# Prompt attention: the softmax weights scaled by diagonals in the turning product, the diagonals built by GpSimd

## The reference, cut to what matters

```python
s = jnp.einsum('bqhgd,bkhd->bhgqk', qf, win_k.astype(f32))
p_win = masked_softmax(s - m * delta.astype(f32), wmask)
o_win = jnp.einsum('bhgqk,bkhd->bqhgd', p_win, win_v.astype(f32))
gate = jax.nn.sigmoid(gts.astype(f32))
o = gate[..., 0:1] * o_cmp + gate[..., 1:2] * o_sel + gate[..., 2:3] * o_win
```

## Time and profile before

| what | us |
| --- | --- |
| median of 3 runs | 2677.11 (2675.2 to 2685.92) |
| the profiled execution, its own time | 2676.88 |
| its span in the trace | 2675.2 |
| TensorE busy in the span | 1895.4 |
| VectorE busy | 1095.8 |
| GpSimd busy | 739.6 |
| ScalarE busy | 439.3 |

### The profile page before, as it was taken

One profiled execution on the slowest core, in us unless ns is written; L12 is line 12 of the kernel. 1 busy time (PEld: TensorE's weight loads), 2 busy tenths in 40 slices (PEclk: granted clock), 3 DMA queues, 4 the chain that ended last, 5 costly groups with the idle time before them and its releaser, 6 DMA issues.

```text
span 2675.2 us, 30528 instructions
## 1 busy us (share of the span) xinstructions
PE 1895.4 (71%) x11821; PEld 1225.1 (46%) x11821; DVE 1095.8 (41%) x1929; ACT 439.3 (16%) x978; POOL 739.6 (28%) x599
## 2 busy tenths in 40 slices
PE   5799999988889934677649897672764116565673
PEld 2477777868768934566536564121221101111120
DVE  2200002426583597676750127018777860000014
ACT  0100000122271212343400101110221000000011
POOL 1000000000010034443452223337546853222234
PEclk8899999999999976787769998766887556777785
DMA  9889997434047689999999999999999999999997
GB/s 385 288 312 347 330 330 239 143 96 156 11 142 233 204 307 416 411 413 412 413 421 402 418 417 417 414 402 405 390 381 410 379 390 406 401 414 421 422 421 315
DMA packets 283277, 911.81 MB, mean 341 GB/s; under 512 B 22254, under 2 KB 158498, under 8 KB 209978
## 3 DMA queue, kind: packets, MB, share of 16 engines
q0 software_dynamic: 78384, 569.78, 52.2%
q1 hardware_dynamic: 176354, 304.77, 32.0%
q10 hardware_dynamic: 28396, 35.35, 3.7%
HBM read 901.18 MB, written 17.21 MB: 343 GB/s over the span
## 4 chain that ended last, share of the span: by engine, by line
DMA 43%; PE 34%; DVE 12%; POOL 7%; issue 3%; ACT 1%; ACTq 0%; SPq 0%; DVEq 0%; POOLq 0%; PEldq 0%
DMA sb_ring<-in_peer_v_dram,sb_modT 19%; DMA sb_ring<-in_peer_u_dram,sb_dist 18%; PE ps L418 14%; POOL sb_ring L2650 7%; DVE sb_ring L2120 4%; PE ps L2572 3%; DMA sb_ring<-in_w_ada_dram 3%; PE ps L212 3%; PE ps L1873 2%; DMA sb_ring<-in_cache_sel_kv_dram 1%; PE ps L2328 1%; PE ps L2291 1%; PE ps L751 1%; PE ps L761 1%; DMA sb_pT<-in_cache_sel_kv_dram 1%
## 5 line engine op out<-in xcount | busy, mean ns | idle before, releaser
L2120 DVE SCALAR_TENSOR_TENSOR sb_ring<-sb_ring,sb_pT 128x2048 f32<-128x2048 f32 x264 | 602.6, 2294 | 244.2 <-DMA sb_ring<-in_peer_u_dram,sb_dist 199.7
L2650 POOL DMA_INDIRECT sb_ring<-in_peer_u_dram,sb_dist x256 | 423.4, 1654 | 532.7 <-DVE sb_ring L2120 352.3
L2572 PE MATMUL ps<-sb_ring,sb_xT 128*32 128x512 f32 x2048 | 343.5, 767 | 192.1 <-DMA sb_ring<-in_peer_v_dram,sb_modT 188.9
L2650 POOL DMA_INDIRECT sb_ring<-in_peer_v_dram,sb_modT x256 | 255.6, 998 | 561.5 <-PE ps L2572 543.7
L418 PE MATMUL ps<-sb_hT,sb_ring 128*128 128x264 f32 x1664 | 374.8, 388 | 0.0
L418 PEld LDWEIGHTS ps<-sb_hT,sb_ring 128*128 128x128 f32 x1664 | 315.5, 190 | 65.3 <-issue 13.0
L2572 PEld LDWEIGHTS ps<-sb_ring,sb_xT 128*32 128x32 f32 x2048 | 49.9, 121 | 426.3 <-DMA sb_ring<-in_peer_v_dram,sb_modT 381.0
L2407 PE MATMUL ps<-sb_ident,sb_ring 128*128 128x128 f32 x512 | 103.7, 359 | 135.9 <-DMA sb_ring<-in_cache_cmp_kv_dram 109.9
L1672 PE MATMUL ps<-sb_work,sb_pT 128*64 128x512 f32 x160 | 99.4, 708 | 98.0 <-ACT sb_work L1560 63.0
L2407 PEld LDWEIGHTS ps<-sb_ident,sb_ring 128*128 128x128 f32 x512 | 78.0, 184 | 159.4 <-DMA sb_ring<-in_cache_cmp_kv_dram 127.9
L2461 ACT ACTIVATE sb_pT<-ps 128x256 f32<-128x256 f32 x256 | 127.5, 661 | 97.0 <-PE ps L2407 96.8
(11 more groups left out here) (586 smaller groups left out, 2383.7 us busy)
## 6 DMA issues: line engine op xcount, KB each, us to landing
sb_ring<-in_w_ada_dram SPq DMA_DIRECT2D x48, 2048.0 KB, 11.1
sb_ring<-in_w_in_dram SPq DMA_DIRECT2D x26, 2048.0 KB, 14.3
sb_ring<-in_peer_wq_dram SPq DMA_DIRECT2D x19, 1024.0 KB, 13.3
sb_ring<-in_cache_cmp_kv_dram SPq DMA_DIRECT2D x68, 256.0 KB, 12.1
sb_ring<-in_w_out_dram SPq DMA_DIRECT2D x8, 2048.0 KB, 8.5
sb_ring<-in_cache_cmp_kv_dram ACTq DMA_DIRECT2D x60, 256.0 KB, 10.6
sb_ring<-in_w_out_dram SPq DMA_DIRECT2D x13, 1024.0 KB, 9.8
sb_pT<-in_peer_wq_dram SPq DMA_DIRECT2D x13, 1024.0 KB, 15.8
```

The source lines that it names most:

```text
L2120: dve.scalar_tensor_tensor(R3(rows), R3(rows), 1.0, h2r[t] if t < NT else R3(h2w), ALU.mult, ALU.mult, accum_out=(dots if t < NT else dots ...
L2572: mm = pe.matmul(bank(G % 2)[32 * q:32 * q + 32, :], w, rows[:, 512 * q:512 * q + 512], start=j == 0, stop=j == last)
L2650: pool.indirect_dma_start(rbuf[e % NBUF], None, io["peer_u" if kind == "u" else "peer_v"][0], bass.IndirectOffsetOnAxis(index, 0)).then_in ...
```

## The change

VectorE no longer scales the weights. It only computes gate / sum for the three branches (for tile 0 the compressed one is also multiplied by the first column of the mask, which is 0 for queries that have no complete block). GpSimd builds from them three diagonal matrices of 128x128 side by side (`dg`, two buffers), as the identity times the three columns. TensorE multiplies the unscaled exponentials by the diagonal of their branch: a product that turns and scales at once, where a transpose against the identity stood. `pool_states` is now called inside GpSimd's loop, behind the diagonals of item 8.

```diff
+        dg = [v3(old(3 * P), 0, 3, P), osq.rearrange("p h c -> p (h c)")[:, 0:3 * P].rearrange("p (r c) -> p r c", r=3)]
@@ pool_att
+            pool.wait_ge(sem("o_sums"), 1)
+            for i in range(N_ATT):
+                pool.wait_ge(sem("p_ready"), i + 1)
+                if i >= 2:
+                    pool.wait_ge(sem("pt_T"), i - 1)
+                pool.tensor_tensor(dg[i % 2], B1(ident[:], 3), B2(stat[1][i % 3], P), ALU.mult).then_inc(sem("diag_ready"), 1)
+                if i == HEADS:
+                    pool_states(pool)
@@ pe_kv
-                pe.wait_ge(sem("p_ready"), i + 1)
+                pe.wait_ge(sem("diag_ready"), i + 1)
                 if i >= 1:
                     pe.wait_ge(sem("pt_moved"), i)
                 for k in range(2 * (t + 1)):
-                    pe.transpose(bank(4 + i % 2)[:, k * P:(k + 1) * P], s[:, k * P:(k + 1) * P], ident[:])
-                pe.transpose(bank(6)[0:NCP, 0:P], s[:, 512:520], ident[:]).then_inc(sem("pt_T"), 1)
+                    pe.matmul(bank(4 + i % 2)[:, k * P:(k + 1) * P], s[:, k * P:(k + 1) * P], dg[i % 2][:, 1 + k // (t + 1), :], start=True, stop=True)
+                pe.matmul(bank(6)[0:NCP, 0:P], s[:, 512:520], dg[i % 2][:, 0, :], start=True, stop=True).then_inc(sem("pt_T"), 1)
@@ dve_kv
                 step(dve, c, dve.reciprocal(total, total))
-                step(dve, c, dve.tensor_tensor(total, total, gates[:, t * 24 + 3 * h:t * 24 + 3 * h + 3], ALU.mult))
-                two = s[:, 0:2 * nk].rearrange("p (a k) -> p a k", a=2)
-                dve.tensor_tensor(two, two, B2(total[:, 1:3], nk), ALU.mult)
-                dve.scalar_tensor_tensor(s[:, 512:520], s[:, 512:520], total[:, 0:1], cseen3[:, t, :], ALU.mult, ALU.mult).then_inc(sem("p_ready"), 1)
+                if t == 0:
+                    step(dve, c, dve.tensor_tensor(total[:, 0:1], total[:, 0:1], cseen3[:, t, 0:1], ALU.mult))
+                dve.tensor_tensor(total, total, gates[:, t * 24 + 3 * h:t * 24 + 3 * h + 3], ALU.mult).then_inc(sem("p_ready"), 1)
@@ gpsimd stream
-            for stage in (pool_setup, pool_att_consts, pool_delta, pool_att, pool_states, pool_samp, pool_peer):
+            for stage in (pool_setup, pool_att_consts, pool_delta, pool_att, pool_samp, pool_peer):
```

More of the change, by code:

```diff
@@ L75 @@
     top_ready exp_done pt_part dve_steps samp_consts samp_ready x1_ready keys_T keys_ready rows_out
-    rows_mm keyscores keyscore_mm halves_done top_diff peer_consts experts_ready ids_here keys_in
+    diag_ready rows_mm keyscores keyscore_mm halves_done top_diff peer_consts experts_ready ids_here keys_in
     rest_in0 w2b_in
```

## The result

The changed kernel takes 2695.93 us (median of 14 runs, 2688.16 to 2708.25) against 2677.65 for the kernel before (14 runs, 2673.82 to 2685.92). The ratio is 1.0071, with a 95% interval of 1.0057 to 1.0084: slower by 19 us (15 to 22), where I had forecast 6 and a range that ended at 2693.

What follows compares the result with a forecast made beforehand. VectorE's work and the round trip between engines, nearly level, were taken to bound the attention stage. First half 1.4, seam 0.1, pause 0.6 and second half 4.05 sum to 6.15 us on 2676.88: 2683 us, range 2675 to 2693.

Steps and rivals of the forecast that it cites:

- What bounds the stage: Prompt attention, second half: VectorE's work (3.66 us a turn) and the round trip through the engines (3.60) are 0.06 apart.
- GpSimd's product: 128x384 diagonal product each turn: 0.87 us, bounds 0.53 to 1.82; gate product to turning 1.15 us instead of 1.08.
- TensorE's term: Turning by full products takes two 0.11 us records each, not one: 0.55 us more a turn, 0.33 in first half.
- First half: Tile 0 of the prompt attention: delays carried head by head make the move behind turning 7 late by 1.4 us.
- Second half at full clock: Tile 1: round trip 4.22 us instead of 3.60, seven turns +4.05 us; its first turn adds +0.1.
- The pause by the state transfers: GpSimd's two DMA issues of the decode states delay the tenth diagonal: +0.6 us, once.
- the states' lateness: States leave some 8.3 us later, delaying output-weight loads, but these arrive before the projection needs them: no cost.
- Sum at full clock: Attention stage: 1.4 + 0.1 + 0.6 + 4.05 = 6.15 us longer.
- The clock: TensorE's granted clock in the attention stage and projection: the forecast had no term for it.
- Pass-through: A shift of the attention stage's end was taken as a shift of the kernel's end, one to one.
- Rival 3: A load or gather behind the attention stage hides its 6 us lengthening: 2677 us; chance 0.15.
- Rival 2: GpSimd's product far slower, at its upper bound or held up by VectorE's traffic: 2693.6 us; chance 0.14.

Runs made afterwards that it cites:

- experiment 6: Kernel before, with TensorE's outputs of the previous item put ahead of the wait for the weights: 2678.00 us, ratio 1.0013 to the kernel before.
- Experiment 1: Kernel before, with turning by full products with the identity instead of transposes, VectorE's scaling kept: 2690.79 us, ratio 1.0047 to the kernel before.
- experiment 5: Changed kernel, with seven unread identity products ahead of TensorE's wait for the diagonals in each of the last two items: 2692.09 us, ratio 1.0054 to the kernel before.
- experiment 2: Changed kernel, with turning by transposes that still wait for GpSimd's unread diagonals, scaling left out: 2686.01 us, ratio 1.0033 to the kernel before.
- 12: Repeat of experiment 2 (changed kernel with transposes kept, scaling left out): ratio 1.0013 to the kernel before.
- experiment 8: Kernel before, outputs first, with outer-product diagonals from the fourth on and the delta heads' output gate moved from VectorE to GpSimd: 2676.32 us, ratio 0.9994.

## Why the prediction was wrong

- *What bounds the stage:* right. VectorE's work and the round trip were level; experiment 6 shows the first, and every item after the change is a round trip.
- *GpSimd's product:* 0.83 us against 0.87, and 1.12 from gate product to turning against 1.15. Right: the slope between the 32 columns of the earlier trace rows and these 384 is 1.67 ns a column, where I had 1.78. In items 14 and 15 the product took 1.03 and 1.01 us, which I had not foreseen. The 2.6 cycles an element of the Trainium skill (GPSIMD Engine Reference, section 3.1) are, as an estimate at the 1.2 GHz that it names, 0.83 us for 384 elements. The trace agrees with that at this size; at 32 columns the same estimate is 0.07 us, where the earlier trace rows have 0.242. My 1.0, from the Trainium skill's figure for 2048 columns in the same section, was too high.
- *TensorE's term:* this is the step that failed first: "five per turn in the second half cost 5 x 0.11 = 0.55 us more". It cost 0.90. I divided the 0.89 us of the chain by eight records, but the chain cuts a group where its neighbour ends. The weight loader's rows were there to be read. Before the change:

```profile
818.91 0.42 PEld L1212 LDWEIGHTS ps<-sb_ident,sb_work 128*128 128x128 f32 x4 [1.72 <-DVE sb_work L1330]
819.30 0.09 PEld L1213 LDWEIGHTS ps<-sb_ident,sb_work 128*8 128x8 f32 x1
819.40 0.97 PEld L1194 LDWEIGHTS ps<-sb_work 128*128 128x128 f32 x8
820.50 0.29 PEld L1195 LDWEIGHTS ps<-sb_work,sb_pT 8*128 8x128 f32 x2
```

Four transposes take 0.39 us and the fifth, of 8 columns, 0.10; four products take 1.10 (819.40 to 820.50). After the change:

```profile
809.73 0.97 PEld L1221 LDWEIGHTS ps<-sb_pT,sb_work 128*128 128x128 f32 x8 [0.48 <-POOL sb_pT L1123]
810.82 0.10 PEld L1222 LDWEIGHTS ps<-sb_pT,sb_work 128*8 128x8 f32 x2
811.13 0.97 PEld L1203 LDWEIGHTS ps<-sb_work 128*128 128x128 f32 x8 [0.22 <-issue]
```

The four turning products take 1.09 and the one of 8 columns 0.31, with the loader idle for 0.22 of it. So a product is 0.27 to 0.31 us against 0.10, 1.40 against 0.49 for the five. Experiment 1 shows it alone: 3.60 + 0.90 = 4.50. The Trainium skill (TensorE: Matmul & The Clock Gate, Terms) calls the transpose mode four times faster for fp32. The trace does not agree: here it is 2.8 times (1.10 us against 0.39 for four).
- *First half:* 2.9 us by the move in item 7, where I had +1.4. The same term, for the most part: turning to outputs grew by 0.68 us, not 0.33 (778.76 to 779.72 by the weight loader's rows, where it was 0.28). Experiment 1, without GpSimd, has 2.0 of the 2.9.
- *Second half at full clock:* seven items took 32.3 us (experiment 5) where they took 25.49, so +6.9, where I had +4.05 and 0.6 for the pause. TensorE's term is 7 x 0.90 = 6.3 of it, and the longer products of GpSimd in the last two items 0.4. Item 8 adds another 0.4, where I had 0.1.
- *The pause by the state transfers:* forecast 0.6, measured 0.13, because the items are longer than the issues; and the states' lateness cost nothing, as forecast.
- *Sum at full clock:* +10.2 in the stage (experiment 5) against +6.15. The mechanism of this part was right and the TensorE term too small.
- *The clock:* missing altogether, and the second step that failed: a term that I had put at nothing without a reason. The stage's end and the projection lost 4.6 + 1.8 us to the lower clock. I had noted that it was 1.00 throughout before, and took that as given for a program with longer waits.
- *Pass-through:* right as far as the timed 19 us show it; the rest is 1792.7 after 1792.6, but moves by up to 9 us from trace to trace. Rival 3 is out, since its time was 2677. Rival 2's time (2693.6) came nearest by luck: GpSimd's product was not slow.
- The two parts make 16.7 us of the measured 19 (15 to 22). The remaining 2 are within the interval, and no run settles whether they are real.

Still open is what makes the clock fall. The length of the waits alone doesn't decide it. The kernel before waits 1.59 and 1.52 us in the last two items and kept the clock at full in both traces; experiment 1 waits 1.53 in each, and its clock fell. The changed kernel waits 1.77 and 1.76, and its clock fell; with transposes kept the waits there are the same, and the clock stayed at full in experiments 2 and 12, while it fell in the middle of the stage, behind a wait of 1.25 us, in all three traces of that form. Experiment 5 shows only that with these waits filled it doesn't fall at the stage's end, in one trace.

## What to carry to other kernels

Where two loops are level, an edit has to shorten both; here the one that was relieved was VectorE's, and the one that was lengthened went through TensorE. A product in place of a transpose costs nearly three times as much here (0.27 us against 0.10 for 128 columns in fp32), and the weight loader's rows show the price of both before the change. Where a hand-over through another engine can't be shortened, first try the order: putting ready work ahead of the wait gave back 12.8 us of 16.7, as much as taking the products out again (experiment 2, 13.0), and it kept the clock. Work moved to an idle engine can slow the engine that it was taken from: look at the durations on both while they run side by side (experiment 8).

## What I had not expected of the hardware

TensorE's clock fell to half for 17 us at the same place in two traces of the same program, with TensorE busy in 14.38 of the 17 us of the second. It cost 1.8 us in a projection that itself has no wait.

GpSimd's product of 128x384 took 0.83 us (0.82 to 0.84) in items 0 to 13 and 1.01 to 1.03 in the last two, in all nine traces that have it, whatever the clock. In these two items VectorE's step of the output gate (L976) starts just before it; in the others it stands behind VectorE's work on the scores:

```profile
826.89 0.49 DVE L976 SCALAR_TENSOR_TENSOR sb_hT<-sb_hT,sb_params,sb_pT 128x264 f32<-128x264 f32 x1
...
827.04 1.03 POOL L1123 TENSOR_TENSOR sb_pT<-sb_ident,sb_small 128x384 f32<-128x384 f32 x1 [3.72 <-DVE sb_small L1338]
```

So VectorE and GpSimd slowed each other where they ran side by side, here by 0.2 us and in experiment 8 by up to 0.48 us an instruction. That the other's instruction is the cause is a reading of these coincidences; no run removes it alone.
